# Gated attention's value products: the context's tiles of both heads first, then the latent tiles

## The reference, cut to what matters

```
def gla_chunked(q, k, v, g, s0):
    def step(s, xs):
        qc, kc, vc, gc = xs
        b = jnp.cumsum(gc, axis=-2)
        rel = b[:, :, :, None, :] - b[:, :, None, :, :]
        rel = jnp.exp(jnp.where(tri[:, :, None], rel, -jnp.inf))
        scores = jnp.einsum('bhid,bhjd,bhijd->bhij', qc, kc, rel)
        o = jnp.einsum('bhij,bhje->bhie', scores, vc) + jnp.einsum('bhid,bhde->bhie', qc * jnp.exp(b), s)
...
def bidir_prefix(scan_f, scan_b, lat_f, lat_b, ctx_f, ctx_b):
    o_cf, s_f = scan_f(*ctx_f, s0)
    o_cb, s_b = scan_b(*flip(ctx_b), s0)
    o_lf, _ = scan_f(*lat_f, s_f)
    o_lb, _ = scan_b(*flip(lat_b), s_b)
    return o_lf + o_lb[:, :, ::-1], o_cf + o_cb[:, :, ::-1]
```

## Time and profile before

| | us |
|---|---|
| median of three runs | 2126.62 (2125.64 to 2127.03) |
| the profiled execution, its own time | 2121.95 |
| its span | 2120.1 |
| mean granted TensorE clock | 0.973 |
| TensorE busy | 1990.2 (94%) |
| VectorE, ScalarE, GpSimd busy | 925.7, 760.1, 738.2 |

### The profile page before, as it was taken

The page is one execution under the profiler, slowest core; times in us unless marked ns, Lnnn a source line. Parts: engine busy times, 40 slices in busy tenths (PEclk is TensorE's granted clock), DMA queues, the critical chain, the costliest instruction groups (busy, mean ns, idle before and its releaser), DMA issues.

```text
span 2120.1 us, 26447 instructions
## 1 busy us (share of the span) xinstructions
PE 1990.2 (94%) x9594; PEld 1668.4 (79%) x9594; DVE 925.7 (44%) x1355; ACT 760.1 (36%) x1062; POOL 738.2 (35%) x324
## 2 busy tenths in 40 slices
PE   4999999999989999878899999999888989999997
PEld 2999999999967875555788888877654857888886
DVE  4633277335453413783411312277875444121124
ACT  4321122112337124553342223355646354232231
POOL 1333233323414221252344443543441313453432
PEclk8999999999999999988999999999989999999999
DMA  8332244334312211001223232341230212332321
GB/s 325 119 124 75 89 149 165 93 110 158 109 50 85 65 50 49 30 1 65 71 89 117 81 109 89 99 129 60 80 109 12 83 55 80 99 109 79 109 89 60
DMA packets 53273, 197.20 MB, mean 93 GB/s; under 512 B 6304, under 2 KB 6864, under 8 KB 51408
## 3 DMA queue, kind: packets, MB, share of 16 engines
q1 hardware_dynamic: 44272, 162.98, 23.9%
q10 hardware_dynamic: 8928, 33.23, 4.4%
HBM read 194.09 MB, written 2.10 MB: 93 GB/s over the span
## 4 chain that ended last, share of the span: by engine, by line
PE 63%; issue 17%; DVE 8%; POOL 7%; ACT 3%; DMA 1%; SPq 1%; POOLq 0%; DVEq 0%; ACTq 0%
PE ps L1845 50%; POOL wlo L531 6%; PE ps L1859 1%; PE ps L1832 1%; PE ps L1834 1%; PE ps L1833 1%; DMA ada_f<-ada_p 1%; PE ps L2154 1%; PE ps L2086 1%; PE ps L2077 1%; PE ps L2248 1%; PE ps L2232 1%; DVE rg_t L1724 1%; DVE rg_h L1728 1%; PE ps L2222 1%
## 5 line engine op out<-in xcount | busy, mean ns | idle before, releaser
L531 POOL TENSOR_TENSOR wlo<-raw,whi 128x1024 fp32r<-128x1024 f32 x280 | 695.9, 2497 | 1303.4 <-ACT whi L567 1281.1
L1845 PE MATMUL ps<-h_hi,whi 128*128 128x512 f32 (+2 forms) x1568 | 510.5, 364 | 13.5 <-issue 5.0
L1845 PE MATMUL ps<-h_hi,wlo 128*128 128x512 f32 (+2 forms) x1568 | 508.1, 363 | 0.0
L1845 PE MATMUL ps<-h_lo,whi 128*128 128x512 f32 (+2 forms) x1568 | 507.4, 362 | 0.0
L567 ACT ACTIVATE whi<-raw 128x1024 fp32r<-128x1024 f32 x280 | 289.2, 1053 | 413.9 <-PE ps L1845 338.9
L1845 PEld LDWEIGHTS ps<-h_hi,whi 128*128 128x128 f32 x1568 | 288.7, 189 | 54.3 <-issue 13.1
L1845 PEld LDWEIGHTS ps<-h_lo,whi 128*128 128x128 f32 x1568 | 288.4, 189 | 33.2 <-issue 1.0
L1845 PEld LDWEIGHTS ps<-h_hi,wlo 128*128 128x128 f32 x1568 | 288.5, 189 | 32.9
L1845 PE MATMUL ps<-g_hi,whi 128*128 128x512 f32 (+1 forms) x784 | 257.4, 364 | 0.0
L1845 PE MATMUL ps<-g_lo,whi 128*128 128x512 f32 (+1 forms) x784 | 257.4, 364 | 0.0
L1845 PE MATMUL ps<-g_hi,wlo 128*128 128x512 f32 (+1 forms) x784 | 257.3, 364 | 0.0
(11 more groups left out here) (405 smaller groups left out, 2277.2 us busy)
## 6 DMA issues: line engine op xcount, KB each, us to landing
raw<-panels SPq DMA_DIRECT2D x280, 512.0 KB, 3.5
ada_w<-ada_t ACTq DMA_DIRECT2D x54, 512.0 KB, 4.3
ada_f<-ada_p SPq DMA_DIRECT2D x8, 1024.0 KB, 18.5
x_lat<-x_t SPq DMA_DIRECT2D x1, 2048.0 KB, 7.7
out<-x_lat SPq DMA_DIRECT2D x8, 256.0 KB, 2.2
x_ctx<-ctx_t SPq DMA_DIRECT2D x1, 1024.0 KB, 9.7
cond_b<-cond SPq DMA_DIRECT2D x1, 1024.0 KB, 23.0
ada_x<-ada_t SPq DMA_DIRECT2D x2, 512.0 KB, 21.3
```

Source lines behind the costliest of these rows:

```text
L531: pool.tensor_tensor(wlo[:, sl], raw[:, sl], whi[:, sl].bitcast(f32), ALU.subtract).then_inc(lo_done, 1)
L1845: ins = pe.matmul(bank(banks + b, n), wt[:, w], a[:, at_(kc, c0):at_(kc, c0) + n], start=kc == 0 and j == 0, stop=kc == n_k - 1 and j == 2)
```

## The change

`values(hp)` computed head 0's six tiles and then head 1's six, behind one wait for all of `s_gla`. Now it waits for the context's tiles alone, computes both heads' context products (two per head), then waits for the rest of `s_gla` and computes both heads' latent products (four per head). The sum of a head begins (`start`) with tile 4 and ends (`stop`) with tile 3. Head 0 is signalled after its last latent product, head 1 after its own.

```
-                    pe.wait_ge(unit_dve, (hp + 1) * MASKED)
-                    pe.wait_ge(unit_act, 4 * (hp + 1))
-                    for a in range(2):
-                        j = 2 * hp + a
-                        for t in range(TILES):
-                            v = gv[:, t * 512 + j * P:t * 512 + (j + 1) * P] if t < LT else gv_c[:, (t - LT) * 512 + j * P:(t - LT) * 512 + (j + 1) * P]
-                            ins = pe.matmul(bank(5 + 2 * a), v, s_gla[:, (a * TILES + t) * LAT:(a * TILES + t + 1) * LAT],
-                                            start=t == 0, stop=t == TILES - 1)
-                        ins.then_inc(o_ready, 1)
+                    pe.wait_ge(unit_act, 4 * hp + 1)
+                    for part in (range(LT, TILES), range(LT)):
+                        if part[0] == 0:
+                            pe.wait_ge(unit_dve, (hp + 1) * MASKED)
+                            pe.wait_ge(unit_act, 4 * (hp + 1))
+                        for a in range(2):
+                            j = 2 * hp + a
+                            for t in part:
+                                v = gv[:, t * 512 + j * P:t * 512 + (j + 1) * P] if t < LT else \
+                                    gv_c[:, (t - LT) * 512 + j * P:(t - LT) * 512 + (j + 1) * P]
+                                ins = pe.matmul(bank(5 + 2 * a), v, s_gla[:, (a * TILES + t) * LAT:(a * TILES + t + 1) * LAT],
+                                                start=t == LT, stop=t == LT - 1)
+                            if part[0] == 0:
+                                ins.then_inc(o_ready, 1)
```

## The result

| | before, us | changed, us |
|---|---|---|
| median, four executions each | 2126.79 (2125.64 to 2127.03) | 2115.32 (2112.58 to 2117.27) |
| ratio, 95% interval | | 0.995 [0.9937, 0.9962] |
| profiled execution, its own time | 2121.95 | 2116.01 |
| its span | 2120.1 | 2114.2 |
| its mean granted clock | 0.973 | 0.971 |

The changed kernel is faster, by 11.5 us in this comparison, where 5.4 us were forecast and 2118.6 us was the range's low end. Two later comparisons of the same two kernels gave 0.9957 [0.9943, 0.9971] and 0.9973 [0.9961, 0.9984]. Over all executions taken as comparison, the changed kernel has a median of 2117.8 us in 19, the one before 2125.7 us in 62: 7.9 us or 0.37%. So the pauses' part was right, the clock's part was larger than forecast, and about a third of the 11.5 was the luck of four executions.

What follows compares the result with a forecast made beforehand. Bound: a chain of waits in gated attention's head pairs, where TensorE pauses for ScalarE's last copy before the value products. From the 2126.6 us median, -2.23 - 2.24 - 0.9 = -5.4 us gave 2121.2 us, range 2118.6 to 2124.4.

Steps and rivals of the forecast that it cites:

- The pauses: TensorE's waits for ScalarE's last copy before each pair's value products, 2.23 and 2.24 us, would be filled wholly: 4.5 us removed.
- What could be late next: Work after the value blocks would not take the pauses' place; the nearest, line 2133 waiting for VectorE's factors, had 2.0 us of room.
- contention: ScalarE's PSUM copies, now beside a working TensorE, would cost zero more, at worst 0.03 us for each of 8.
- the added wait: The new wait for the context's copy before the value products would cost nothing but its issue.
- The clock: Half of the 1.70 us lost to half clock in the second value block would return: 0.9 us, bounds 0 to 3.5.
- The base: The gain was taken off the runs' median, 2126.62 us, 4.7 us above the profiled execution.
- Only one of the two pauses: Rival: something with less room takes the first pair's pause, so 2.24 us remain: 2124.4 us; chance 0.13.
- The shift is eaten elsewhere: Rival: moving later work by 4.5 us brings two more clock falls over TensorE-bound work: 2125.5 us, no change; chance 0.14.
- Interleaved order holds the array at half clock: Rival: alternating banks in the value products runs both blocks at 1.2 GHz: 2140.1 us; chance 0.06, shared with a third fall.

Runs made afterwards that it cites:

- order_only: Changed kernel with the whole wait of the kernel before put back ahead of all value products, so the pauses stay; 2126.91 us, ratio 0.9999 to the kernel before.
- no_context: Kernel before without the context's value products of gated attention, its order, waits and pauses kept; 2118.95 us, ratio 0.997 to the kernel before.
- filler: Kernel before with two added products of a context tile, their result overwritten, inside each pause; 2122.55 us, ratio 0.9991 to the kernel before.
- only_second: Kernel before with the new order of value products in the second head pair only; 2120.50 us, ratio 0.998 to the kernel before.
- before_again: The kernel before, unchanged, measured again as a kernel of its own; 2125.62 us, ratio 0.9997 to the kernel before.
- only_first: Kernel before with the new order of value products in the first head pair only; 2120.51 us, ratio 0.9973 to the kernel before.
- hold_tail: Changed kernel with unread products added where TensorE idles: one before the norm's sums, two before their spread; 2115.48 us, ratio 0.9953 to the kernel before.

## Why the prediction was wrong in size

**The pauses: right.** Both are gone, 2.23 and 2.24 us; "TensorE finds the last copy done about 1.2 us before" was 1.4. The first head's copy came 7.1 us after the last unit and no longer 7.7, the second's 10.5 instead of 12.8, as worked out. order_only shows that it is the overlap and not the order, and no_context that a microsecond taken off here arrives as a microsecond.

**What could be late next, contention, the added wait: right.** No wait of line 2133 or 886 took the pause's place, and the copies kept their 592 to 618 ns.

**The clock: the step that failed.** "I take half of the one fall seen, 0.9 us." What the pauses leave is 7.9 - 4.5 = 3.4 us, by the first comparison even 7. Of these, about 2.2 us lie in the stage, as filler and only_second show with one trace each: 1.7 are the fall over the block, 0.3 to 0.5 are line 2163 (2.29 us in the earlier trace rows, 2.46 in before_again, 1.96 now). The fall was in both traces of the kernel before, in order_only and in no_context, so halving it was wrong. What line 2163 gains I had not counted; it is not the tail of that fall but the start of the next one, which the sums now escape by ending earlier. The reason given for the half, that the stretches shift, was not empty: only_first lost the fall by a shift, with its pause in place. What decides where a fall lies stays open; the place of the pause behind the clock's last rise is the one sign the traces give. The stage as a whole lost 6.6 us on average, 2.1 more than the pauses, which agrees. The last 1.3 us lie outside the stage; the means of 62 and 19 executions differ by 7.9 with a standard error of 0.7, so the 1.3 are not clear of noise. That time at half clock went from 126 to 120 us points to the clock there as well, but no experiment placed it.

**The base: the second step that failed.** "Three runs of the kernel lie within 1.4 us" was taken for its spread. It is 9 us wide over 62 executions, 11.5 with those of before_again. The median of three, 2126.6, is 0.9 above that of 62 executions; the changed kernel's first median, 2115.3, is 2.4 below that of 19. Together they make 3.4 of the 5.9 us between forecast and result; the clock makes the other 2.5 (3.4 instead of 0.9). The bounds of the clock (0 to 3.5 us) just held the settled 3.4; the range in us was too narrow because it had no term for how far executions of one kernel lie apart.

**The rivals.** "Only one of the two pauses" would have given 2124.4 us; both arrived. "The shift is eaten elsewhere" had the wrong sign: the shift of only_first took a fall away and added none. "Interleaved order holds the array at half clock" was tried by itself in order_only and fell.

The rule of the Trainium skill (TensorE: Matmul & The Clock Gate, Part 1), that idleness brings the clock down and work holds it up, would have given 2120.4 us and was the better guide. filler (0.50 to 1.00 over the block) and hold_tail (the spread 2.00 us instead of 3.45 to 3.80) agree with it; only_first and the five first pairs, with a pause and no fall, show that a pause of 2.2 us does not always do it.

## What to carry to other kernels

When TensorE waits for a copy of its last operands, issue first the products whose operands are ready: here the pause came off the chain whole, since they outlast it, and their order cost nothing. Count a fall of the clock that follows a pause fully if it lies over TensorE-bound work and repeats; take more than one trace to see whether it does. Where another engine sets the pace, holding the clock gained nothing here. Before giving a range, ask how far executions of one kernel lie apart: three of this one agreed within 1.4 us where the spread is 9 or more.

## What the runs showed of the hardware

- Two products that nobody reads (1.7 us of work) in a pause of 2.2 us went with a granted clock of 1.00 over the next 10 us. With that pause idle it fell to 0.50 over the next work in four of five traces; the fifth is only_first. The kernel with more work was 1.9 us faster (0.9991 [0.9982, 0.9999]).
- A kernel whose instructions are the same spreads with the granted clock: 2119.6 to 2129.1 us in 62 executions on two chips, 0.22 us more per us at half clock (correlation 0.81).
- Float32 products of 128x512 whose two sums stay open in two banks at once (2, 2, 4 and 4 products in turn) cost what they cost one sum after the other: 24 records in 10.55 us either way in the first pair, 0.9999 [0.999, 1.0007] in time.
